# Retention with each head's values behind its own rows, and the block compression spread over four gaps

## What is computed

```python
# first block, twice: half FFN, mixer of four branches, half FFN
u = rmsnorm(h, norm_g[l, 1]); cols = u @ w_in[l]
y_a = mla_mixer(...); y_b = swa_mixer(...); y_c = nsa_mixer(...); y_d = diff_mixer(...)
merged = sum(sigmoid(u @ w_gate[l, b]) * (y_b @ w_branch[l, b]))      # four branches
h = h + merged @ w_o[l]
# inside nsa_mixer, for keys and for values: 15 windows of 32 tokens
blocks = take(t, idx, axis=2) + pos_emb
hdn = gelu(blocks.reshape(..., nc, 32 * 64) @ w1); kcmp = hdn @ w2
# second block: layer 0 dilated attention, layer 1 retention, each between two FFNs
q, k = rotary(q), rotary(k) * DK_R ** -0.5                             # 4 heads of 256
inner = (q @ k.T) * decay_mask        # forward and backward, values 512 wide
y = silu(g_f) * group_norm(y_f) + silu(g_b) * group_norm(y_b)
out = y.reshape(S, 2048) @ w_out
```

## Time and profile before

| | |
|---|---|
| median of 3 runs (lowest, highest) | 3003.28 us (3002.51, 3003.71) |
| profiled execution, its span | 3002.07 us, 3000.3 us |
| TensorE busy | 2831.6 us (94%) |
| VectorE, ScalarE, GpSimd busy | 1792.7, 1345.9, 88.5 us |
| mean granted TensorE clock | 0.974 |
| DMA | 488.4 MB, 163 GB/s in the mean |

### The profile page before, as it was taken

One profiled execution on the slowest core, in us unless ns is written; L12 is line 12 of the kernel. 1 busy time (PEld: TensorE's weight loads), 2 busy tenths in 40 slices (PEclk: granted clock), 3 DMA queues, 4 the chain that ended last, 5 costly groups with the idle time before them and its releaser, 6 DMA issues.

```text
span 3000.3 us, 41146 instructions
## 1 busy us (share of the span) xinstructions
PE 2831.6 (94%) x16502; PEld 2415.3 (81%) x16502; DVE 1792.7 (60%) x2749; ACT 1345.9 (45%) x1939; POOL 88.5 (3%) x135
## 2 busy tenths in 40 slices
PE   7999899999999989999999989998999998997998
PEld 6888788788788878887878889995887878883687
DVE  5666466366666546645676665554666665542566
ACT  5443344254454434434455544444555453440444
POOL 1000000000000000000001001110000000000000
PEclk9999899999999989999999999999999999998999
DMA  6544333445454533335555544443554553442453
GB/s 240 186 183 148 115 139 127 154 172 187 163 188 186 188 128 109 144 148 204 188 187 182 186 157 164 165 165 123 185 187 154 189 189 147 147 148 73 159 189 119
DMA packets 49042, 488.40 MB, mean 163 GB/s; under 512 B 6480, under 2 KB 6576, under 8 KB 10520
## 3 DMA queue, kind: packets, MB, share of 16 engines
q1 hardware_dynamic: 43192, 470.44, 42.6%
q0 software_dynamic: 5728, 16.25, 1.8%
HBM read 485.47 MB, written 1.19 MB: 162 GB/s over the span
## 4 chain that ended last, share of the span: by engine, by line
PE 83%; DVE 8%; ACT 5%; issue 2%; DMA 1%; POOL 0%; DVEq 0%; ACTq 0%; SPq 0%; POOLq 0%
PE ps L803 64%; PE ps L857 15%; ACT ring_hi L1413 3%; DVE ring_lo L1745 3%; PE ps L819 1%; PE ps L1067 1%; DMA norm_g<-norm_gT_dram 1%; DVE ring_lo L1814 1%; PE ps L1264 1%; PE ps L1278 1%; PE ps L1173 0%; ACT ring_hi L1461 0%; DMA ring<-stream_dram 0%; DVE h L1851 0%; DVE work_all L1970 0%
## 5 line engine op out<-in xcount | busy, mean ns | idle before, releaser
L803 PE MATMUL ps<-uT,ring_hi 128*128 128x512 f32 (+1 forms) x5536 | 1524.4, 347 | 24.9 <-DVE qkT L1866 11.1
L803 PE MATMUL ps<-uT,ring_lo 128*128 128x256 f32 x4176 | 1179.6, 282 | 0.0
L803 PEld LDWEIGHTS ps<-uT,ring_hi 128*128 128x128 f32 x5536 | 963.6, 192 | 178.5 <-issue 19.4
L803 PEld LDWEIGHTS ps<-uT,ring_lo 128*128 128x128 f32 x4176 | 798.2, 191 | 6.2
L1814 DVE TENSOR_TENSOR ring_lo<-ring,ring_hi 128x2048 fp32r<-128x2048 f32 x174 | 398.8, 2292 | 240.4 <-ACT ring_hi L1461 240.4
L1745 DVE TENSOR_TENSOR ring_lo<-ring,ring_hi 128x3072 fp32r<-128x3072 f32 (+1 forms) x100 | 297.2, 2973 | 269.4 <-ACT ring_hi L1413 269.4
L1413 ACT ACTIVATE ring_hi<-ring 128x3072 fp32r<-128x3072 f32 (+1 forms) x100 | 245.5, 2455 | 316.8 <-PE ps L803 162.0
L1461 ACT ACTIVATE ring_hi<-ring 128x2048 fp32r<-128x2048 f32 x174 | 330.6, 1900 | 0.0
L857 PE MATMUL ps<-ring_hi,hid_hi 128*128 128x512 f32 x704 | 276.9, 393 | 9.7 <-DVE hid_lo L1809 9.7
L803 PE MATMUL ps<-ring_hi,uT 128*128 128x384 f32 (+1 forms) x1024 | 264.9, 338 | 15.0 <-DVE ring_lo L1745 9.9
L857 PE MATMUL ps<-ring_lo,hid_hi 128*128 128x512 f32 x704 | 276.0, 392 | 0.0
(11 more groups left out here) (271 smaller groups left out, 2500.1 us busy)
## 6 DMA issues: line engine op xcount, KB each, us to landing
ring<-stream_dram SPq DMA_DIRECT2D x299, 1536.0 KB, 6.3
mlaT_all<-bias_vectors POOLq DMA_DIRECT2D x32, 96.0 KB, 2.8
bias<-gains_dram POOLq DMA_DIRECT2D x5, 512.0 KB, 7.2
yR<-bias_vectors POOLq DMA_DIRECT2D x1, 2048.0 KB, 10.9
mlaT_all<-bias_vectors POOLq DMA_DIRECT2D x32, 64.0 KB, 3.0
row<-ret_const_dram POOLq DMA_DIRECT2D x1, 1280.0 KB, 5.7
h<-x_rows_dram POOLq DMA_DIRECT2D x2, 512.0 KB, 11.5
yR<-gains_dram POOLq DMA_DIRECT2D x2, 512.0 KB, 9.5
```

The source lines that it names most:

```text
L803: m = pe.matmul(out_, lhsT, rhs, start=start, stop=stop, **kw)
```

## The change

- **Compression.** w1's first half stays in slot 9, slot 10 now holds tiles 12 to 14, slot 11 the second half and w2. The 64 matmuls are made in four groups of 16, one behind each piece of steps 1 and 2. Each half is an accumulation of its own; VectorE copies the first out and adds the second (`take_hidden`). GELU is one activation at step 3; all later parts move one step back.
- **Splits in attention.** The split of slot 10 is made in step 0, behind exponentials and `normalise`. Those of steps 3 and 5 to 19 move forward: on ScalarE to the start of the step, on VectorE to right behind `bias_max`. Step 2's stays.
- **Retention.** TensorE's order per head becomes: scores, its own rows, `turn` of the head before, values. The last head's values go to banks 4 to 7; blocks 0 to 3 of the output projection come ahead of them, 4 to 11 behind them, then the last `turn` and blocks 12 to 15. VectorE rotates head 0 behind the fourth q/k copy and the others between the copies and splits of head 0's rows; statistics and gating of head h come beside the rows of head h + 1. `gated_head` gets a wait for the transposes of the head before.

```diff
-T_SLOTS = [4, 5, 7, 8, 11, 12, 13]
+T_SLOTS = [4, 5, 7, 8, 10, 12, 13]
...
-        SPLIT_STEPS = {2: 12, 3: 13} | {t: t + 9 for t in range(5, 20)}
+        SPLIT_STEPS = {0: T_SLOTS[4], 2: 12, 3: 13} | {t: t + 9 for t in range(5, 20)}
+        LATE_SPLITS = (0, 2)
...
+                if t in (1, 2):
+                    if t == 1 and gap == 0:
+                        pe.wait_ge(blocks_ready, l + 1)
+                    if gap == 0:
+                        weights(c1)
+                    for l_ in range(8 * gap, 8 * gap + 8):
+                        pos_ = (t - 1) * 16 + l_
+                        for w in range(2):
+                            r = slice(64 * w, 64 * w + 64)
+                            last = mm(ps[:, 2 + w, 0:2 * NC], slot(c1)[r, l_ * P:(l_ + 1) * P],
+                                      blk[r, pos_, :, :], l_ == 0, l_ == 15, skip_group_check=True)
+                    if gap:
+                        last.then_inc(cmp_hidden, 1)
...
             def turn(l, t):
-                if t == 2:
-                    pe.wait_ge(cmp_gelu, l + 1)
-                if t == 3:
+                if t in (2, 3):
+                    pe.wait_ge(cmp_taken, 2 * l + t - 1)
+                if t == 4:
                     pe.wait_ge(cmp_kv_out, l + 1)
...
+                for hh in range(RH):
+                    inner_scores(hh)
+                    rows_of(hh)
+                    if hh:
+                        turn(hh - 1)
+                    if hh == RH - 1:
+                        for n in range(2):
+                            pe.wait_ge(*piece_copied(ret_piece("turn", 0, n)))
+                        project(range(0, 4))
+                    inner_values(hh)
+                for n in range(2):
+                    pe.wait_ge(*piece_copied(ret_piece("turn", RH - 2, n)))
+                project(range(4, 12))
                 turn(RH - 1)
...
+                project(range(12, 16))
...
             def attention(l):
                 for t in range(STEPS):
+                    compress(l, t)
+                    if t in SPLIT_STEPS and t not in LATE_SPLITS:
+                        take_high(mix_slot(l) + SPLIT_STEPS[t])
                     if 1 <= t <= PAIRS:
                         copy_pT(l, t - 1)
...
+                copies("qk")
+                for hh in range(RH):
+                    inner_weights(hh)
+                    if hh:
+                        statistics(hh - 1)
+                    copies("rows", hh, range(0, 2))
+                    if hh:
+                        gated_head(hh - 1)
+                    else:
+                        rotate_head(1)
+                    copies("rows", hh, range(2, 4))
+                    if hh == 0:
+                        rotate_head(2)
+                    copies("rows", hh, range(4, 6))
+                    if hh == 0:
+                        rotate_head(3)
+                    copies("rows", hh, range(6, 8))
+                    if hh:
+                        copies("turn", hh - 1)
+                statistics(RH - 1)
+                gated_head(RH - 1)
+                copies("turn", RH - 1)
...
-                take_low(c0 + T_SLOTS[4])
...
+            def take_hidden(l, t):
+                dve.wait_ge(cmp_hidden, 2 * l + t)
+                x = ps[:, 2:4, 0:2 * NC]
+                if t == 1:
+                    dve.tensor_copy(hidC[:, :, :], x).then_inc(cmp_taken, 1)
+                    dve.wait_ge(cmp_taken, 2 * l + 1)
+                else:
+                    dve.tensor_tensor(hidC[:, :, :], hidC[:, :, :], x, ALU.add).then_inc(cmp_taken, 1)
...
                     if t < PAIRS:
                         bias_max(l, t)
+                    if t in SPLIT_STEPS and t not in LATE_SPLITS:
+                        take_low(mix_slot(l) + SPLIT_STEPS[t])
                     if t:
                         add(2 * t - 1)
                     if t < PAIRS:
                         normalise(l, t)
+                    if t in SPLIT_STEPS and t in LATE_SPLITS:
+                        take_low(mix_slot(l) + SPLIT_STEPS[t])
                     if t == 13:
                         diff_norm(l, 1)
-                    if t in SPLIT_STEPS:
-                        take_low(mix_slot(l) + SPLIT_STEPS[t])
```

More of the change, by code:

```diff
@@ L449, in build, with ret_piece, ret_banks @@
         PIECES_RET = PIECES_DIL + 8 * 8
[L450 to L454, removed]
+        RET_PIECES = [("qk", t) for t in range(16)]
+        for hh in range(RH):
+            RET_PIECES += [("row", hh, n) for n in range(8)] + [("turn", hh - 1, n) for n in range(2) if hh]
+        RET_PIECES += [("turn", RH - 1, n) for n in range(2)]
+        def ret_piece(*what):
+            return PIECES_RET + RET_PIECES.index(what)
+        def ret_banks(hh):
+            return 1 if hh + 1 < RH else 4
         def dilated_copy(g):
@@ L1160, in finish_merge, with out_project @@
                             (merged, 32 * l + branches_before(32) + 1))
[L1162 to L1164 removed]
+            def out_project(c0, lhs, nk, blocks=None, ks=None):
+                for k in range(nk) if ks is None else ks:
                     c = c0 + k // 3
@@ L1528, in retention, with copies @@
                 take_high_back(c0 + 1)
-                at_piece = [PIECES_RET]
-                def copies(n):
-                    for _ in range(n):
-                        copy_2(at_piece[0], retention_copy)
-                        done_retention(at_piece[0], take_high)
-                        at_piece[0] += 1
+                def copies(what, *which):
+                    for n in range({"qk": 16, "row": 8, "turn": 2}[what]):
+                        g = ret_piece(what, *which, n)
+                        copy_2(g, retention_copy)
+                        done_retention(g, take_high)
                 def decay(hh):
@@ L1917, in retention, with copies @@
             def retention(p):
-                at_piece = [PIECES_RET]
-                def copies(n):
-                    for _ in range(n):
-                        copy_2(at_piece[0], retention_copy)
-                        done_retention(at_piece[0], take_low)
-                        at_piece[0] += 1
-                copy_row(p, 5)
-                dve.wait_ge(ret_const_in, 16)
-                copies(16)
-                s, v = piece_copied(PIECES_RET + 15)
-                dve.wait_ge(s, v)
+                def copies(what, *which):
+                    for n in range({"qk": 16, "row": 8, "turn": 2}[what]) if what != "rows" else which[1]:
+                        g = ret_piece("row", which[0], n) if what == "rows" else ret_piece(what, *which, n)
+                        copy_2(g, retention_copy)
+                        done_retention(g, take_low)
+                        if what == "qk" and n == 3:
+                            rotate_head(0)
                 t = [xn_flat[:, 512 * n:512 * n + 512].rearrange("p (a t) -> p a t", a=2) for n in range(4)]
@@ L1942, in retention, with inner_weights @@
                     dve.wait_ge(ret_rotated, hh + 1)
-                copies(8)
-                for hh in range(RH):
+                def inner_weights(hh):
                     dve.wait_ge(ret_exp, hh + 1)
@@ L1981, in retention @@
                     dve.wait_ge(ret_head, hh + 1)
-                copies(2)
+                copy_row(p, 5)
+                dve.wait_ge(ret_const_in, 16)
+                copies("qk")
+                for hh in range(RH):
+                    inner_weights(hh)
[13 more added lines that the diff above has]
+                    copies("rows", hh, range(6, 8))
+                    if hh:
+                        copies("turn", hh - 1)
+                statistics(RH - 1)
+                gated_head(RH - 1)
+                copies("turn", RH - 1)
             def final_norm():
```

154 lines of the change are left out of this document (67 added, 87 removed).

## The result

The changed kernel takes 2922.5 us (median of 4 runs, 2916.6 to 2926.5) where the kernel before took 3002.9 beside it: a ratio of 0.973 (95% interval 0.971 to 0.975). The forecast was 2919. By medians the gain is 80.4 us; from profiled execution to profiled execution it is 3002.07 to 2919.25, so 82.8 us against a forecast of 83.7. TensorE is busy 96% of the span now instead of 94%.

A forecast was written before the change was run, and what follows sets the result against it. TensorE bounds it, busy 94% of the span, losing time standing still and at the lower clock level. Attention 46.3 + retention 44.4 - moved splits 6 - clock 1 = 83.7 us; 3003.3 - 84 = 2919 us, range 2906 to 2944.

The forecast's parts named there:

- Attention, steps 0 to 5: Both attention layers: standing and slow-clock time removed, 22.7 us gained in layer 0 and 23.6 in layer 1, 46.3 together.
- the first turn: Attention step 1: the first transpose, 9.55 us late before, starts at 306.4 without a wait.
- tile 9's copy: Attention step 0: queued behind slot 10's split on VectorE, it makes tile 11 wait, a new 1.35 us.
- the 61.5 us: Layer 0, from 299.22 to step 6's transpose: summed work and the new wait, against 84.2 us before.
- the transfer of layer 0's sum to layer 1: Layer 1 waited 10.4 us instead of 9.55, so its gain was taken as 23.6 us against 22.7.
- rival 3: Attention's first wait stays because slot 10 lands as late as slot 11 did: 26 us lost, 2945 us; chance 0.05.
- Moved splits: Attention steps 5 to 19: the add queued behind the split frees its bank late, about 3 us a layer, 6 lost.
- Retention: From the q/k copies to the projection's end: 2750.4 instead of 2794.9, 44.4 us gained, less 1 for the clock.
- Rival 1: Attention steps 1 to 5: the clock dips behind each of four small groups, 13 us lost, 2932 us; chance 0.13.
- Rival 2: Retention heads 1 to 3: gating 3 us late on VectorE delays splits, 15 us lost, 2934 us; chance 0.12.
- Rival 4: Rebuilt stretches: TensorE stays at the lower clock and the kernel gets slower, 3032 us at 35%; chance 0.02.
- The drain: Table switches: about 1.38 us each by the skill, making turn 4 wait 1.4 us a layer; left out.

The follow-up runs named there:

- split0_only: Kernel before, with only slot 11's split moved from the end of the projections to step 0, weights still in slot 11: 2992.9 us, ratio 0.996.
- late_splits: Changed kernel with the splits of steps 5 to 19 back behind normalisation on VectorE and the output copies on ScalarE: 2921.9 us.
- proj_end: Changed kernel with the whole output projection of retention behind the last head's transpose: 2945.8 us, ratio 0.980.
- two_blocks: Changed kernel with the compression's passes in two blocks of 64 at the ends of steps 1 and 2, instead of four groups of 32: 2930.6 us.
- block_early: Changed kernel with two blocks of 64 compression passes, each ahead of the second tile of steps 1 and 2: 2928.4 us.
- queue_attn: Changed kernel with VectorE's branch add ahead of the split (steps 7 to 19) and tile 9's copy ahead of step 0's split: 2908.3 us, ratio 0.968.
- best: Changed kernel with both VectorE reorderings (attention, q/k copies), plus VectorE copying the first half of turned outputs of heads 0 to 2: 2902.6 us, ratio 0.966.
- queue_qk: Changed kernel with retention's q/k splits one copy later on VectorE and head 0's rotation behind the sixth copy: 2915.8 us, ratio 0.970.

## Why the prediction was right

The gain was right within 1 us of that of the profiled execution (82.8 for 83.7), and within 4 us by the medians (80.4). The mechanisms were right, the closeness was partly luck: the gain in attention was 4.8 us too high and that in retention 1.3, and the loss by the moved splits some 5 us too high, and these cancelled; and the profiled execution is one in which the clock kept at 1.00 behind waits that cost some of it in others.

- **Attention, steps 0 to 5** (forecast 46.3): 21.5 us in layer 0 and 20.0 in layer 1, 41.5. The mechanisms were those named: the first turn, tile 9's copy, GELU and normalisation in time. In layer 0 the 61.5 us were 62.7, with no wait that was not foreseen. The mis-sized term is the tile: 2.88 us is its pace behind another tile, and with other work on both sides it took 3.06, so that twelve took 36.6 us and not 34.6; the four small groups gave back 0.4 (7.6 for 8.0), the turns 0.3. The longer tiles also left step 4's turn 0.9 us in hand (its last copy ended at 341.74), where I had reckoned none. The sum adds 0.4 us of overlaps, where an overlap shortens a sum. Layer 1 took 65.4. The step that failed there is the transfer of layer 0's sum to layer 1: it left out the table load (1.2 us more of waiting) and the clock behind the longer wait. `split0_only` shows that the wait was half queue, half load; that the new slot would remove the load's half was the argument against rival 3.
- **Moved splits** (forecast 6 lost): the two large waits came where forecast, at step 18 0.99 us (forecast 1.25) and at step 19 2.71 (2.9); those at the seven steps with 0.2 us did not show, and one of 0.85 us in step 14 was not foreseen. What failed is the other side of the account: the kernel before waited 1.5 us in step 14, 1.3 ahead of the next turn and 2.2 in step 20, 4.9 us in layer 0 against 5.3 now. `late_splits`, where these waits are back, shows it. I had counted 2.6 back.
- **Retention** (forecast 44.4 less 1 for the clock): 42.1. Rotation 1.21 for 1.35, the first row piece 1.82 for 2.0, values of head 0 0.72 for 0.75. The 1 us for the clock behind the 1.82 was not lost in this execution, by chance: in five of nine kernels with this wait the clock did fall behind it. What the sum lacked are waits in the first rows of heads 2 and 3 for ScalarE's copy of a turned output, 0.70 and 0.69 us, and some length in three terms: scores 1.0 us, rows 0.7, projection 0.8. (The turns took 5.0 us, their small waits of 0.23 us included; the sum has 5.8, though four at its 1.3 are 5.2.) That copy stands behind a table load and a swish. It is the same queue that `proj_end` showed at 3.26 us.
- **Rival 1** (the clock between small groups): not here, 1.00 in steps 0 to 6 of layer 0. But that small passes can cost the clock is real, as the two kernels with blocks of 64 show, so a chance of 0.13 was not too much. The Trainium skill (TensorE: Matmul & The Clock Gate, "A second HAM failure mode: psum-queue depth-cycling") puts such swings down to short idles between groups of matmuls; here the alternating groups of 32 kept the clock, and blocks of 64 lost it with no idle time in the windows shown, which does not rule out rests inside a block that the profile cannot show.
- **Rival 2** (VectorE late in retention): no wait for ring_lo in heads 1 to 3. **Rival 3**: in layer 0's step 0 no DMA releases ScalarE's split any more. **Rival 4**: never near.
- The drain that the Trainium skill (ScalarE: Activation LUTs, "What ACT_TABLE_LOAD costs") adds to a table load was rightly left out. In the rows above the load starts at 1049.19 and its activation at 1050.49, 1.30 us later. The turn of step 4, which by the forecast's reckoning would have waited 1.4 us, waited for nothing in either layer; with 0.9 us in hand in layer 0 that alone would be weak evidence.

## What to carry to other kernels

When a wait sits behind an in-order engine, ask for each operation in that queue who needs it soonest, and put bulk work that itself waits (here the splits) behind the small copies that free a bank; two such reorderings, with no operation added, gave 14.3 and 6.8 us more by the medians. When a wait is moved, count what disappears at its old place as carefully as what appears at the new one. A stage that repeats in another layer is not the same stage: look at what its first steps need that the other layer had already, such as a table.

## What the runs showed of the hardware that I had not expected

- The granted clock can fall where the profile shows no standing of TensorE: behind 3.8 to 4.5 us of 64-row, 30-column passes it was 0.50 to 0.72 with 4.00 of 4.00 us busy, in three of four blocks in each of two kernels; behind groups of 32 (1.97 us) it did not, in 64 groups of eight profiled executions.
- The length of a single wait near 2 us does not say whether the clock falls behind it. The same wait in the profiled executions of the kernels of this document, with the mean granted clock of the 4 us behind it:

| wait | clock 1.00 | clock fell |
|---|---|---|
| 1.82 us, first row piece of retention | 4 (changed, `late_splits`, `two_blocks`, `block_early`) | 5, to 0.58 to 0.65 |
| 2.51 us, tile 11 of layer 1 | 2 (`two_blocks`, `block_early`) | 6, to 0.50 to 0.64 |
| 2.71 us, step 19, both layers | 4 of 14 (two of them the changed kernel's) | 10, to 0.50 to 0.68 |

- So the reading of the earlier trace rows in the prediction, 2.29 us with a fall and 1.94 without, was one draw of each and no bound between them. By a rough estimate, 4 us at a mean of 0.6 do the work of 2.4 us, so each fall costs some 1.6 us.
- The changed kernel's runs spread over 10 us and those with blocks of 64 over 9.5 and 12, where `queue_attn` and `best` spread over 2. I take the difference for clock dips that come in some executions only, since the table shows such dips; but one execution of each kernel was profiled, and `queue_qk`, with the 2.51 and 2.71 us waits still in it, spread over 2.5, so what decides it stays open.
